# A two-block transformer kernel: bonus sum later in the merge loop, convolution taps earlier, another order in the tail of the RWKV mixer, and throwaway products on TensorE

## What is computed

```python
r, k, v, d_w, d_a, d_g = split_cols(p, [...])          # 256 x 512 each
y = rwkv7_scan(r, decay, k, v, kk, a)                  # 8 heads of 64: S_t = S_{t-1} diag(w_t) - ..., y_t = S_t r_t
y = groupnorm(y) * lnx_g + lnx_b
bonus = sum(r * k * r_k over a head) * v
y_a = (y + bonus) * g
conv = depthwise_conv(c_val * sigmoid(c_gate), 31 taps) + conv_b
y_b = silu(layer_norm(conv, ...))
return concatenate([y_a, y_b]) @ w_out                 # then x = x + rms_norm(...)
```

## Time and profile before

| | us |
|---|---|
| median of 3 runs (2462.99 to 2463.59) | 2463.41 |
| the profiled execution's own time | 2461.77 |
| its span, first to last instruction | 2460.0 |
| TensorE busy (97% of the span) | 2397.1 |
| VectorE busy (59%) | 1460.8 |
| ScalarE busy (44%) | 1071.3 |
| GpSimd busy (5%) | 121.6 |

### The profile page before, as it was taken

The page is one execution under the profiler, slowest core; times in us unless marked ns, Lnnn a source line. Parts: engine busy times, 40 slices in busy tenths (PEclk is TensorE's granted clock), DMA queues, the critical chain, the costliest instruction groups (busy, mean ns, idle before and its releaser), DMA issues.

```text
span 2460.0 us, 29664 instructions
## 1 busy us (share of the span) xinstructions
PE 2397.1 (97%) x11572; PEld 1979.5 (80%) x11572; DVE 1460.8 (59%) x1598; ACT 1071.3 (44%) x1308; POOL 121.6 (5%) x145
## 2 busy tenths in 40 slices
PE   8999999999999999999999999998999999999998
PEld 7888877888888888788878887887888888787887
DVE  5445766654654666685455456895545545645544
ACT  4443455444344444554444444423444444545442
POOL 0001000000000100000000002111000000100000
PEclk9999999999999999999999999998999999999999
DMA  8565535565555654355555565204555556343552
GB/s 271 190 218 200 182 103 178 182 205 187 188 188 188 223 186 167 120 205 195 189 188 186 185 220 181 69 1 137 182 190 196 184 188 206 119 141 129 194 187 88
DMA packets 281235, 426.56 MB, mean 173 GB/s; under 512 B 11747, under 2 KB 193635, under 8 KB 281136
## 3 DMA queue, kind: packets, MB, share of 16 engines
q1 hardware_dynamic: 273632, 400.04, 49.1%
q0 software_dynamic: 7520, 25.37, 3.2%
HBM read 422.49 MB, written 1.05 MB: 172 GB/s over the span
## 4 chain that ended last, share of the span: by engine, by line
PE 85%; DVE 11%; ACT 2%; issue 1%; POOL 1%; DMA 0%; SPq 0%; DVEq 0%; POOLq 0%; ACTq 0%
PE bank L1895 25%; PE bank L1897 25%; PE bank L1896 25%; DVE wl L1117 4%; PE bank L2345 2%; PE bank L2037 1%; PE bank L1942 1%; POOL rstd L463 1%; DVE stats L1152 1%; DVE x L1161 1%; PE bank L2140 1%; DVE y L1186 1%; DVE arena L1614 0%; DVE y L1219 0%; PE bank L1949 0%
## 5 line engine op out<-in xcount | busy, mean ns | idle before, releaser
L1117 DVE TENSOR_TENSOR wl<-wf,wh 128x2048 fp32r<-128x2048 f32 x355 | 808.4, 2289 | 419.7 <-ACT wh L622 419.2
L1895 PE MATMUL bank<-wh,xTh 128*128 128x512 f32 x2336 | 929.5, 398 | 16.2 <-DVE wl L1117 7.6
L1897 PE MATMUL bank<-wh,xTl 128*128 128x512 f32 x2336 | 913.4, 391 | 0.0
L1896 PE MATMUL bank<-wl,xTh 128*128 128x512 f32 x2336 | 912.2, 391 | 0.0
L622 ACT ACTIVATE wh<-wf 128x2048 fp32r<-128x2048 f32 x355 | 673.2, 1915 | 250.6 <-PE bank L1897 248.3
L1895 PEld LDWEIGHTS bank<-wh,xTh 128*128 128x128 f32 x2336 | 441.9, 189 | 110.7 <-issue 11.3
L1897 PEld LDWEIGHTS bank<-wh,xTl 128*128 128x128 f32 x2336 | 441.0, 189 | 93.9
L1896 PEld LDWEIGHTS bank<-wl,xTh 128*128 128x128 f32 x2336 | 442.0, 189 | 87.5 <-issue 0.7
L1895 PE MATMUL bank<-wh,hTh 128*128 128x512 f32 x704 | 277.0, 393 | 0.1
L1897 PE MATMUL bank<-wh,hTl 128*128 128x512 f32 x704 | 274.9, 390 | 0.0
L1896 PE MATMUL bank<-wl,hTh 128*128 128x512 f32 x704 | 274.5, 390 | 0.0
(11 more groups left out here) (328 smaller groups left out, 1501.8 us busy)
## 6 DMA issues: line engine op xcount, KB each, us to landing
wf<-in_ffn_w SPq DMA_DIRECT2D x160, 512.0 KB, 4.8
wf<-in_w_in SPq DMA_DIRECT2D x52, 1024.0 KB, 5.4
wf<-in_ffn_w SPq DMA_DIRECT2D x44, 1024.0 KB, 5.0
wf<-in_ffn_w_down SPq DMA_DIRECT2D x44, 1024.0 KB, 5.1
wf<-in_ffn_w_gate SPq DMA_DIRECT2D x80, 512.0 KB, 4.0
wf<-in_ffn_w_up SPq DMA_DIRECT2D x80, 512.0 KB, 4.9
wf<-in_w_branch SPq DMA_DIRECT2D x16, 1024.0 KB, 5.2
wf<-in_c_w_in SPq DMA_DIRECT2D x14, 1024.0 KB, 5.7
```

The lines of the kernel that those rows point to most:

```text
L1117: dve.tensor_tensor(wl[s], wf[s], wh[s].bitcast(f32), ALU.subtract).then_inc(SEM[f"lo{s}"], 1)
L1895: pe.matmul(o, lh, rh, start=start, stop=False)
L1896: pe.matmul(o, lh, rl, start=False, stop=False)
L1897: return pe.matmul(o, ll, rh, start=False, stop=stop)
```

## The change

- **Merge loop (DVE).** The bonus sum moves from step 8 to step 21, behind the last taps. `taps_at` gives two taps in place of one in steps 18 and 20 and none in 22 and 23. `conv_done` is given in step 21. `centred(0)` comes ahead of the end of step 23.
- **Tail.** DVE: `spread(0)` ahead of the convolution's statistics, `gated_y(0)` and `out_x(0, 1, 6)` ahead of `centred(1)`. POOL: the power for heads of b = 0 ahead of the two for the convolution. ACT: the copy of u behind `y_squares(0)`, and the order of `silu_conv`, `out_x` and `y_squares(1)` altered. TensorE: the transposes of the convolution's second block behind the first `part_unit`.
- **Way out.** ACT: `prep(0, 2)` behind `new_square_sum(0)` and `take_x(0)`; DVE: `low(0)` behind `take_x(0)`.
- **Throwaway products (TensorE).** `busy(n, bank, t)` issues n float32 products of 128 by 128 whose results nothing reads: 12 of zeros ahead of `start_ld` (DVE clears `sil[:, 0, 0:P]` first), 18 of the identity after the transposes of `first_head`, 14 and 4 in the tail.

```diff
+        power(h_rstd[:, 0:8], h_sum[:, 0:8], 8, "head_var", "head_rstd")
         for b in range(TB):
             norm(b)
-        for b in range(TB):
-            power(h_rstd[:, 8 * b:8 * b + 8], h_sum[:, 8 * b:8 * b + 8], 8, "head_var", "head_rstd")
+        power(h_rstd[:, 8:16], h_sum[:, 8:16], 8, "head_var", "head_rstd")
...
-        taken(u_s, 1, 4, "u_mm", "u_ready")
...
         y_squares(0)
-        for b in range(TB):
-            silu_conv(b)
+        taken(u_s, 1, 4, "u_mm", "u_ready")
+        silu_conv(0)
+        out_x(0, 1, 6)
+        silu_conv(1)
         y_squares(1)
-        out_x(0, 1, 6)
+        out_x(0, 0, 4)
         out_x(1, 1, 7)
-        out_x(0, 0, 4)
         out_x(1, 0, 5)
...
-        out_of_mixer(RMS)
+        square_sum(0)
+        new_square_sum(0)
+        take_x(0)
+        prep(0, 2)
...
+        dve.memset(sil[:, 0, 0:P], 0.0).then_inc(SEM["zeros"], 1)
...
+        def taps_at(i):
+            if i < 2 or i > 21:
+                return 0
+            return 2 if i > 3 and (i % 2 or i in (18, 20)) else 1
...
-            if i == 8:
+            if i == 23:
+                centred(0)
+            if i == 21:
+                first_state()
+            for _ in range(taps_at(i)):
+                tap(j)
+                j += 1
+            if i == 21:
+                assert j == CONV
+                dve.wait_ge(SEM["dve"], c.so_far("dve"))
+                dve.sem_inc(SEM["conv_done"], 1)
                 dve.wait_ge(SEM["rk_made"], c.next("rk_made"))
                 dve.tensor_reduce(bonus, r_t.rearrange("p b (h n) -> p (b h) n", n=HD), X, ALU.add).then_inc(SEM["bonus_done"], 1)
-            if i == 21:
-                first_state()
-            for _ in range(0 if i < 2 else 2 if i % 2 and i > 3 else 1):
-                if j < CONV:
-                    tap(j)
-                    j += 1
...
-        centred(0)
+        spread(0)
         dve.wait_ge(SEM["convT"], c.next("convT", TB))
         for b in range(TB):
             conv_stats(b)
-        spread(0)
...
+        gated_y(0)
+        out_x(0, 1, 6)
         centred(1)
-        gated_y(0)
         spread(1)
-        out_x(0, 1, 6)
+        out_x(0, 0, 4)
         out_x(1, 1, 7)
-        out_x(0, 0, 4)
         gated_y(1)
         out_x(1, 0, 5)
         low(4)
         low(5)
         full = RmsNorm(1.0)
-        out_of_mixer(full)
+        full.variance(0)
+        full.scaled(0)
+        full.pre_variance(0)
+        full.pre_scaled(0)
+        take_x(0)
+        low(0)
...
+        def busy(n, bk, t):
+            for _ in range(n):
+                pe.matmul(bank[bk][:, 0:P], t, t, start=True, stop=True)
+
         def first_head():
             turn(0, x, None)
             turn(1, x, None, (2, 3))
+            busy(18, 0, ident[:, :])
             x_in()
...
+        pe.wait_ge(SEM["zeros"], c.next("zeros"))
+        busy(12, 0, sil[:, 0, 0:P])
         pe.wait_ge(SEM["start_ld"], c.next("start_ld", 16 * 2))
...
-        for b in range(TB):
-            pe.wait_ge(SEM["yb_ready"], c.next("yb_ready"))
-            turn_half(y_conv[:, b, :], 6 + b)
+        busy(14, 1, ident[:, :])
+        pe.wait_ge(SEM["yb_ready"], c.next("yb_ready"))
+        turn_half(y_conv[:, 0, :], 6)
+        busy(4, 1, ident[:, :])
         pe.wait_ge(SEM["ya_ready"], c.next("ya_ready"))
         turn_half(y_rwkv[:, 0, :], 4)
         x_in()
         part_unit(1, 1, 0, 0, True, False)
+        pe.wait_ge(SEM["yb_ready"], c.next("yb_ready"))
+        turn_half(y_conv[:, 1, :], 7)
         part_unit(2, 1, 0, 1, True, False)
```

More of the change, by code:

```diff
@@ L215, in new @@
         names.extend(ns)
-    new("held", "start_ld", "const_ld", "warm", "first_hi", "first_lo", "half", "pre_var", "pre_rstd")
+    new("held", "start_ld", "const_ld", "warm", "zeros", "first_hi", "first_lo", "half", "pre_var", "pre_rstd")
     for s in range(SLOTS):
@@ L1643, in take_gram, with centred @@
                    .then_inc(SEM["gram_made"], 1)
+        def centred(b):
+            dve.wait_ge(SEM["y_mm"], c.next("y_mm"))
+            s, o = h_sum[:, 8 * b:8 * b + 8], bank[2 + b][:, :]
+            settle(dve.tensor_reduce(s, heads(o), X, ALU.add))
+            settle(dve.tensor_scalar(s, s, -1.0 / HD, None, ALU.mult))
+            dve.tensor_tensor(heads(y_rwkv[:, b, :]), heads(o), per_head(s), ALU.add).then_inc(SEM["yc_ready"], 1)
         def first_state():
@@ L1677, in _ @@
                 take_gram(i - 2)
[L1678 to L1687, removed]
         def spread(b):
```

## The result

The changed kernel takes 2438.61 us (median of 4 runs, 2437.47 to 2440.91); the kernel before took 2463.2 beside it (4 runs, 2462.79 to 2463.59). The ratio is 0.9901, 95% interval 0.9884 to 0.9919: faster by 24.6 us. The forecast was 2443.6 with a range from 2440 to 2449, so the time lies 5.0 under the forecast and 1.4 under the range. The profiled execution's own time is 2437.79, its span 2436.0 (2460.0 before), its granted clock 0.996 (0.988 before).

The account below looks back on a forecast made before the run. TensorE, 85% of the chain, was taken as the bound. Gains of 8.5 + 3.1 + 6.8 + 1.5 = 19.9 took 2461.77 to 2441.9; with 1.6 for the runs' median, 2443.6 us, range 2440 to 2449.

Parts of the forecast that it names:

- what is gained stays: Outside the edited stretches: TensorE sets the pace and nothing is edited, so no gain is lost; counted at nothing.
- part 1: Merge loop, steps 8 to 11: with the bonus moved, POOL no longer delays DVE's taps; gain 8.5 (8.3 to 8.6).
- Part 2: Merge loop's end, steps 18 to 23: the added taps and bonus sum make TensorE late; cost 1.0 (0 to 2.1).
- none has two large SBUF operands: Loop's end: two masks, `centred(0)` and `spread(0)` beside POOL's products are not held up; cost nothing.
- Part 3: Tail: first product 2.1 sooner, a 1.1 stall for `gated_y(1)`, throwaways cost nothing; gain 3.1, Part 2's 1.0 counted.
- Part 4: Way out: ACT's 6.95 wait behind `prep(0, 2)` goes; 7.2 sooner, 0.4 late afterwards, net 6.8 (4.5 to 7.2).
- Part 5: Start: products of zeros raise the clock, transposes take 1.8, the 18 throwaways end at 12.5; gain 1.5.
- A: Start and tail: the clock falls all the same, start -0.1 for 1.5, tail -2; 2447, chance 0.2.
- B: Tail or merge loop: POOL's products collide with the tail, or the loop doesn't keep 7.47; 2446 to 2448, chance 0.1.
- C: Way out: only the wait is gained, something else being late, 4.5 or less; 2446 to 2449, chance 0.11 with E.
- E: Orders don't do what they say, another wait keeps ACT's 6.95; 2450, chance 0.11 together with C.
- D: From the start on: extra products leave TensorE at half clock for long, slower; 2474 with 60 us, chance 0.02.

Follow-up runs that it names:

- the filler run: The changed kernel with four throwaway TensorE products added in each of merge steps 10 and 11: 2442.43 us, 0.9925 of the kernel before.
- the second comparison: The changed kernel again with no edit, timed against the kernel before, both profiled a second time: 2440.64 us, ratio 0.9917.

## Why the prediction came out as it did

The direction and the mechanism of each part held; the time did not fall in the range. The step that failed is "Outside these stretches nothing is edited and TensorE sets the pace, so what is gained stays": it puts everything outside at nothing. The profiled execution gained 24.0 where the sum gave 19.9. Of these 4.1, 1.2 belong to part 1, whose term was too small, 3.0 to the clock in stretches that I counted at nothing (1.65 and 1.3 in the table), and the rest, -0.1, to all the others. The 0.2 between the first Silu and 392 isn't a fall of the clock, as neither execution has one there; it goes with the start's edit: the stretch takes 369.78 to 369.89 in all five executions without the zeros, 369.52 to 369.59 in the nine with them. A slip of the forecast itself: 2441.9 and 1.6 are 2443.5, not 2443.6.

**Part 1, the mis-sized term.** "Two pairs take 7.47 twice, or 7.2 and 7.5 ...: 14.7" took the pace of steps 6 to 8 for that of steps 8 to 12. They took 14.34, and the pairs behind them 7.14 and 6.69 where they had taken 7.48 and 7.15. Steps 10 and 11 are of the last level, which leaves out half of the merge products (`if merge_level(i) < 6`), so TensorE runs ahead. Before, this lead vanished in the wait for POOL; now DVE, at 7.15 a pair, is what both wait for up to the mask of step 14. 8.54 + 0.34 + 0.46 + 0.36 = 9.70, measured 9.68. Filling the lead gave back 1.13 of it (the filler run). The hold of 7.3 and the sum of 1.1 are measured at 7.26 and 1.09.

**The range, the step that failed.** "What is gained stays" holds for the work, not for the clock. A fall of the granted clock costs about 1.6, and which falls a profiled execution has differs between executions of one program: the kernel before has one at 13.6 in one execution, and in another runs its first 13 products at half pace; the one at 396 is absent with the loop's edit alone, and present with the filler in steps 10 and 11. The start's and the middle's falls could each give 1.6 or take it, and my lower end of 2440 held bounds of the edited stretches alone. The times of the kernel before show the same spread: 2463.4, where I began, is above all of 2456.1 to 2463.25. By the ratio of the second comparison, 0.9917, the gain is 20.4, by the first 24.6. The two intervals overlap from 0.9904 to 0.9919; how the whole gain splits between the edits and the clock elsewhere isn't settled closer than that. The second pair of profiled executions gives 3.2 outside the edited stretches too, partly in other places: 1.6 at 392 to 403, 1.5 from there to the merge loop, -0.9 and 1.0 behind 2130. But in both pairs the profiled execution of the changed kernel is one of its shorter ones (2437.79 and 2438.18), and that of the kernel before one of its longer. The edited stretches of the first pair give 21.0 (24.0 less 3.0), close to the 20.8 between the medians of the second comparison. That speaks for chance in the 3.0, but doesn't prove it; why a fall comes in one execution and not in another stays open.

**Part 2.** 0.9 given back at the loop's end for a forecast 1.0. The masks (0.69) and the reductions (0.69) kept their time beside POOL's products, as "none has two large SBUF operands" wants. That rule is too narrow: L1703, 128 by 8 with one input, took 1.63 beside them and 0.17 away from them. It cost nothing, since DVE waits 1.80 for TensorE behind it.

**Part 3.** Statistics to the first product 7.96 for 8.0; TensorE waits 0.79 for `gated_y(1)` for a forecast 1.1; the powers took 1.67 for 2.1. The gain on the stretch is 4.0 for 4.1. The throwaways lengthened nothing, as forecast, and the full clock that they keep is 1.7 of the 4.0.

**Part 4.** 7.2 for 7.2. The turn comes 0.39 behind TensorE's arrival (forecast 0.4). What comes late behind it is 0.7, not 0.4: `low(0)` stands behind DVE's variances, and the old order gets 0.6 back there.

**Part 5.** The transposes took 1.97 for 1.8, the throwaways ended at 12.50 for 12.5, the first product came at 12.79 where it was at 12.54. The gain is 1.3 for 1.5, since the clock stays up from there. In the second pair of executions it is 2.1, because the kernel before ran its first 13 products at half pace.

That transposes "raised" the clock doesn't hold for every execution. Behind the same 16 transposes, with nothing else ahead, the granted clock reads full from 10.2 in the execution that the prediction read and from 9.6 in the one without throwaways at the start. In the second execution of the kernel before and in the one with the loop's edit alone the first products run at 0.43, to 18.2 and 15.5. Without the zeros the transposes run at 0.22 each, and with them ahead at 0.12. The Trainium skill, TensorE: Matmul & The Clock Gate, Part 4: PE-mode transpose, says that the full clock doesn't engage for transposes. The 1.97 shows them at full pace once products have raised the clock. By themselves they were followed by a full clock in two of four executions, which the page's rule doesn't account for; what decides it these runs don't show.

**The rivals.** A (the clock falls at the start and in the tail): it fell in neither; without the throwaways the tail's fall is there, at 1.7. B (POOL's products collide with the tail): not so with the sum in step 21, as the loop's edit alone shows, whose tail is at 11.07 as before; with the sum two steps later, in step 23, it came true, at 3.7. C and E (the way out gains less): refuted by 7.2 and by the old order, which takes back 7.0 of it. D (slower by a long stretch at half clock): the changed kernel's record has 13.7 us at half clock, the kernel before's 51.2, both without the last 6 us of the span and the first microseconds, which have no record.

## What to carry to other kernels

Price an added or a moved step by the pace of its own pair of steps: look up which steps have less work, because the engine that is ahead keeps its lead until it meets a wait, and taking a stall away gives that lead back too. POOL's products with SBUF operands belong beside instructions that read PSUM; moving one reduction of 1.1 us by thirteen steps was worth 9.7. Where the granted clock falls at several places by chance, put one fall (1.6 here) for each of them into the range on both sides, and compare with many runs of the kernel before.

## What the runs showed of the hardware

- While POOL ran products on SBUF, a DVE scalar operation on 128 by 8 with one SBUF input took 1.63 and 1.42 (0.17 undisturbed), and another, L1653, 0.32. Each ended 0.03 after one of POOL's products did (L1703 at 1659.53, the product at 1659.50). One on 128 by 1 kept its 0.15 beside the products in the run with the sum in step 23. Reductions from SBUF (0.69) and masks from PSUM (0.69) kept their time. The Trainium skill, SBUF — State Buffer, Who interferes with whom, says that of a DVE operation in a mode that uses two ports and a GpSimd instruction the one that comes second fully blocks until the first is done. The held scalar operations, which end as POOL's product ends, agree with it if they ran in such a mode, which no run shows.
- 12 products of zeros ahead of the transposes raised the clock: 16 transposes took 1.97 with them and 3.67 without.
- Which short falls of the granted clock occur (some 1.6 us lost by each) differs between executions whose program up to there is the same.
